# Routing tables filled four columns at a time, an earlier place in the load queue for the input projection's first columns, and a key-norm spread by transposes

## The chip, the core and the metric

The kernel runs on one NeuronCore of one Trainium2 chip. A core has a matrix engine (TensorE, PE in the rows), a vector engine (VectorE, DVE), an activation engine (ScalarE, ACT), a general engine (GpSimd, POOL), and a sync engine (SyncE, SP) that issues most of the transfers. The metric is the device time of one execution in microseconds; lower is better.

## The reference

One layer over 1024 tokens of width 1024: an adaptive norm, one input projection whose columns feed two mixers (a recurrent one with 8 heads and a sparse attention with 8 heads), an output projection, then an adaptive norm and a mixture of 32 experts of which every token takes 2, and a last adaptive norm.

```python
shift1, scale1, gate1, shift2, scale2, gate2 = jnp.split(c_act @ ada_w[l] + ada_b[l], 6, axis=-1)
h = modulate(rms_norm(x, norm1_g[l]), shift1, scale1)
proj = h @ w_in[l]
...
kk = heads(k * k_k)                                   # recurrent mixer: the key, per head
kk = kk / jnp.maximum(jnp.sqrt(jnp.sum(kk * kk, axis=-1, keepdims=True)), 1e-12)
...
order = jnp.argsort(expert)                           # experts: the assignments, sorted by expert
counts = jnp.bincount(expert, length=N_EXPERTS)
padded = (counts + MOE_BLOCK - 1) // MOE_BLOCK * MOE_BLOCK
pend = jnp.cumsum(padded)
dest = (pend - padded)[s_exp] + jnp.arange(n_assign) - start[s_exp]
row_tok = jnp.zeros((n_rows,), jnp.int32).at[dest].set(s_tok)
```

## The kernel before

The program is one straight list of instructions for each engine, with semaphores between them (`sig` raises one, `wait_ge(*at(...))` waits for it, `link` raises one and lets the same engine wait for it). `step` is a `link` of an engine to itself, so that a chain of `step`s is strictly one after the other. There are four stages.

**Project.** SP queues the 8 tiles of x, then the first two of eight conditioning vectors' weights: `load_vector(0)` into slots 0 and 1 of four weight slots, `load_vector(1)` into slots 2 and 3, 2 MB each slot. PE turns x into `hT`, multiplies the conditioning vector by both (`ada`, signal `ada_done`), and DVE and ACT apply scale and shift to `hT` in 16 pieces of 512 columns (`h_even` on DVE, `h_odd` on ACT; the first four of each are the first half of the tokens). Meanwhile `load_group(0)` fetches the first 452 columns of `w_in` into slot 0 in two transfers, 68 columns (`narrow_loaded`) and 384 columns. It waits until PE has read slot 0, and for the landing of the second vector (`slot_loaded3`). The first projection (L801, "rows", one group of 16 matmuls for each of 8 token tiles) needs both transfers and the first half of `hT`; from then on PE works through the other column groups, and DVE, ACT and POOL search the top 256 keys of each query with what it gives. POOL builds constants in this time, among them `steps`, and issues the small loads once the second vector is there. The stage ends with a barrier of all engines.

**Mix.** Eight token tiles of 128 are worked off one after the other. `prepare(t)` normalizes the keys of the next tile: POOL makes the reciprocal norms, DVE spreads them over the head's columns in `rnb` (L1178), PE brings them from rows to columns in bank T1 (L1400, `kk_spread`), DVE multiplies (L1184). Just ahead of that PE turns the values into bank T0 (L1395), ACT empties T0 (L1042), and just behind it PE writes the gate into T0 (L1405). The stage ends with a barrier.

**Route.** Output projection, second norm, choice of the experts. At its end a chain without other work: PE sums up ranks and counts (`ranks`, L1903); DVE works out how many blocks of 32 rows each expert gets (at least 2), each assignment's place `dest`, and two tables: `in_row` (16 columns of tokens x 32) and `in_block` (16 x 132). PE multiplies them (L1907, signal `rows_found`), which gives the token in each row of each block. DVE turns that into the row indices `idx_all` (`indices_ready`), and POOL gathers the first blocks' rows with them. `first_block` holds the first block of every expert (`bounds_ready`).

**Experts.** The blocks go through gate, up and down projections on PE (L2181, L2192). SP loads the 6 MB of an expert into one of three slots as soon as PE has finished with the expert that was in it. Then both rows of each token are added and normalized.

```python
if g == 0:                                            # load_group, SP
    sp.wait_ge(*at("slot_loaded3", "ada", 1))
...
step(dve.tensor_tensor(more, over(counts, SEQ // BLK - 2), each(steps[:, :], NE), ALU.is_gt))
step(dve.tensor_reduce(last, more, AX_X, ALU.add))
```

Of the kernel before, what the change touches and what calls it, by code (L numbers as in the profile page):

```python
# [27 lines left out]
P = 128  # L28
# [24 lines left out]
BLK = 32  # L53
QUARTERS = P // BLK
QD = D // QUARTERS
SLOTS = 3
MAX_BLOCKS = 2 * NE + 2 * SEQ // BLK
# [81 lines left out]
def sparse_attention_moe_layer(nc, x, c, ada_w, ada_b, norm1_g, w_in, shift_mu, w0, w_decay_up, a0, w_aaa_up,  # L139
# [3 lines left out]
    with ExitStack() as ctx:  # L143
        def sb(name, shape, dt=F32):
            return ctx.enter_context(nc.sbuf_tensor(name, shape, dt))
# [52 lines left out]
        steps = sb("steps", [P, SEQ // BLK - 2])  # L198
# [54 lines left out]
        with ExitStack() as scope:  # L253
# [68 lines left out]
            def _(sp):  # L322
# [22 lines left out]
                def load_group(g):  # L345
# [5 lines left out]
                    if g == 0:  # L351
                        sp.wait_ge(*at("slot_loaded3", "ada", 1))
# [36 lines left out]
            def _(pool):  # L389
# [75 lines left out]
                for i in range(SEQ // BLK - 2):  # L465
                    step(pool.memset(steps[:, i:i + 1], float(BLK * (i + 2))))
# [375 lines left out]
        with ExitStack() as scope:  # L842
# [474 lines left out]
            def _(pe):  # L1317
# [59 lines left out]
                def prepare(t):  # L1377
# [21 lines left out]
                    for p in range(NPAIR):  # L1399
                        mm = pe.matmul(g4(psum["T1"])[:, p, :], g4(rnb)[:, p, :], ident[:, :], start=True, stop=True)  # L1400
# [215 lines left out]
        with ExitStack() as scope:  # L1616
# [19 lines left out]
            more, nblk, last, begin = A.take(NE, SEQ // BLK - 2), A.take(NE + 1), A.take(NE), A.take(NE)  # L1636
# [88 lines left out]
            def _(dve):  # L1725
# [98 lines left out]
                step(dve.tensor_copy(first_block[:, 0:NE + 1], nblk))  # L1824
                blocks, pairs = first_block[:, NE:NE + 1], first_block[:, NE + 1:NE + 2]
                step(dve.tensor_scalar(pairs, blocks, 1, None, ALU.bitwise_and))
                step(dve.tensor_tensor(blocks, blocks, pairs, ALU.add))
                step(dve.tensor_scalar(pairs, blocks, 1, None, ALU.logical_shift_right))
                dve.tensor_scalar(first_block[:, NE + 2:NE + 3], pairs, 2, None, ALU.subtract).then_inc(bounds_ready, 1)
                dve.wait_ge(bounds_ready, 1)  # L1830
# [13 lines left out]
                step(dve.tensor_tensor(in_row, over(place_f[0], BLK), each(count_f[:, 0:BLK], 2 * NT), ALU.is_equal))  # L1844
                step(dve.tensor_tensor(in_row, in_row, over(pair_f.rearrange("p t j -> p (t j)"), BLK), ALU.mult))
# [142 lines left out]
            def _(pool):  # L1988
# [6 lines left out]
                for j in range(2):  # L1995
                    gather_first(j)
# [275 lines left out]
```

## Time and profile before

| | |
|---|---|
| median of 3 runs | 1739.64 us (1739.58 to 1743.02) |
| the profiled execution, its own time | 1740.19 us |
| its span (first to last instruction) | 1738.4 us |
| granted TensorE clock, mean over the span | 0.93 of full speed |
| PE busy, share of the span | 87% |
| DVE, ACT, POOL busy, share of the span | 50%, 33%, 26% |

The profile is of one execution. Busy shares are means over stages with different limits, so each stage is read by itself. In a row of the timeline the first number is when a run of alike instructions starts (us from the span's start), the second how long it lasts in all, and the brackets hold the idle time of that engine ahead of it and what ended it. "PEld" is the weight load of PE, "SPq" an issue of a transfer by SP.

### The profile page before, as it was taken

To read this page: it belongs to the slowest core of one execution; us is meant where nothing else is said; L and a number is where in the kernel's file an instruction comes from. 1 tells how busy PE (TensorE), PEld (TensorE's weight loads), DVE (VectorE), ACT (ScalarE), POOL (GpSimd) and SP (SyncE) were. 2 spreads that over 40 slices of the span, in tenths; PEclk is the share of its full clock that TensorE was granted. 3 is DMA by queue.
4 is the path that set the end of the run, shared out by engine and by line. 5 is a ranking of instruction groups with operands and counts; after the bars stand their busy time and mean duration, and the time that the engine had idled before them with its cause. 6 is when DMAs were issued, how large, how long until landed. Compare 5 with 4: busy or idle time off the path is not lost. (4 is left out here: it accounts for less than half of the span.)

```text
span 1738.4 us, 45781 instructions
## 1 busy us (share of the span) xinstructions
PE 1511.5 (87%) x18148; PEld 933.1 (54%) x18149; DVE 874.5 (50%) x1937; ACT 567.4 (33%) x1264; POOL 450.7 (26%) x971
## 2 busy tenths in 40 slices
PE   4799999986778788788889999579889999999976
PEld 3644444434566666666667455535445555555542
DVE  3347578534467766867765332623223333333327
ACT  3212897761324344445445121111111111111122
POOL 6500457740101110110110000033333333343331
PEclk9899999998778898899899999589999999999998
DMA  9613443232020211011003473579999999999945
GB/s 325 209 37 130 173 179 115 93 133 85 1 41 24 86 48 41 14 41 42 8 27 105 145 266 109 218 262 405 408 407 407 392 400 379 406 407 365 407 165 241
DMA packets 136144, 336.71 MB, mean 194 GB/s; under 512 B 14500, under 2 KB 56748, under 8 KB 134992
## 3 DMA queue, kind: packets, MB, share of 16 engines
q1 hardware_dynamic: 126752, 316.09, 48.4%
q0 software_dynamic: 9264, 18.86, 3.2%
q8 instruction: 87, 1.43, 0.3%
q14 instruction: 41, 0.34, 0.1%
HBM read 303.09 MB, written 37.25 MB: 196 GB/s over the span
## 5 line engine op out<-in xcount | busy, mean ns | idle before, releaser
L2181 PE MATMUL psX<-arena 128*32 128x256 f32 x5376 | 331.2, 387 | 15.4 <-DMA arena<-in_e_up_dram 10.4
L2181 PEld LDWEIGHTS psX<-arena 128*32 128x32 f32 x5376 | 166.9, 111 | 136.0 <-issue 43.0
L2192 PE MATMUL psP<-arena 128*32 128x256 f32 x2688 | 160.7, 379 | 10.1 <-issue 9.6
L523 ACT ACTIVATE arena<-arena 128x1024 bf16<-128x1024 f32 (+5 forms) x138 | 134.4, 974 | 31.1 <-POOL arena L481 27.2
L824 PE MATMUL psX<-arena 128*128 128x512 f32 x320 | 140.9, 595 | 3.5 <-DVE arena L730 2.0
L824 PE MATMUL psP<-arena 128*128 128x512 f32 x320 | 141.2, 595 | 3.1 <-DVE arena L730 1.6
L2091 DVE TENSOR_TENSOR arena<-arena,pair_cols 128x256 f32<-128x256 f32 x85 | 36.2, 426 | 199.6 <-PE psX L2181 199.6
L2192 PEld LDWEIGHTS psP<-arena 128*32 128x32 f32 x2688 | 88.3, 110 | 68.7 <-issue 14.7
L2052 ACT ACTIVATE arena<-psX 64x256 f32<-64x256 f32 x84 | 31.7, 378 | 251.8 <-PE psX L2181 251.8
L2011 POOL DMA_INDIRECT arena<-xn_rows,arena x84 | 88.3, 1051 | 74.0 <-POOL arena L2008 70.5
L2021 POOL DMA_INDIRECT expert_rows<-arena x84 | 85.8, 1021 | 74.1 <-POOL arena L2018 74.1
L824 PEld LDWEIGHTS psP<-arena 128*128 128x128 f32 x320 | 59.9, 190 | 80.2 <-issue 75.4
L824 PEld LDWEIGHTS psX<-arena 128*128 128x128 f32 x320 | 60.0, 190 | 78.9 <-issue 73.7
L2085 DVE TENSOR_TENSOR arena<-psT,pair_cols 128x256 f32<-128x256 f32 x85 | 36.1, 425 | 119.7 <-PE psT L2159 119.7
L479 POOL TENSOR_SCALAR arena<-arena 128x1 f32<-128x1 f32 x132 | 58.3, 441 | 145.8 <-ACT arena L523 138.7
L2056 ACT ACTIVATE arena<-psW 128x128 f32<-128x128 f32 x84 | 23.3, 278 | 209.9 <-PE psW L2164 209.9
L952 POOL TENSOR_TENSOR st<-st,mhalf 128x8 f32<-128x8 f32 x16 | 29.1, 1818 | 174.6 <-DVE st L1193 91.4
L1531 PE MATMUL psW<-arena 64*64 64x64 f32 x1280 | 51.4, 237 | 22.9 <-DVE arena L1273 22.8
L1147 DVE CUSTOM_DVE_ANT_0 arena<-psP,arena 128x384 f32<-128x384 f32 (+5 forms) x48 | 42.8, 891 | 53.9 <-PE psP L1330 53.0
L1531 PEld LDWEIGHTS psW<-arena 64*64 64x64 f32 x1280 | 46.0, 150 | 33.0 <-DVE arena L1273 29.8
L2008 POOL COPY arena<-idx_all 128x1 int32 (+1 forms) x84 | 15.6, 186 | 185.5 <-ACT arena L2048 185.5
L980 POOL TENSOR_TENSOR arena<-arena,ident 128x512 f32<-128x512 f32 x8 | 9.0, 1123 | 206.9 <-DVE arena L1297 183.7
(442 smaller groups left out, 2723.9 us busy)
## 6 DMA issues: line engine op xcount, KB each, us to landing
arena<-in_e_gate_dram SPq DMA_DIRECT2D x32, 2048.0 KB, 14.2
arena<-in_e_up_dram SPq DMA_DIRECT2D x32, 2048.0 KB, 18.3
arena<-in_e_down_dram SPq DMA_DIRECT2D x32, 2048.0 KB, 17.2
arena<-in_ada_w_dram SPq DMA_DIRECT2D x12, 2048.0 KB, 14.3
proj_T<-arena SPq DMA_DIRECT2D x36, 256.0 KB, 2.0
arena<-in_x_dram SPq DMA_DIRECT2D x16, 512.0 KB, 6.5
arena<-in_w_in_dram SPq DMA_DIRECT2D x4, 2048.0 KB, 9.0
arena<-in_final_ada_w_dram SPq DMA_DIRECT2D x4, 2048.0 KB, 10.3
```

The costliest lines, as they stand in the source:

```text
L479: step(pool.tensor_scalar(s_hit[k], s_sum[k], s_lim[k], s_step[k][:, i - 1:i], ALU.is_gt, ALU.mult))
L523: link(act, act.activation(junk_bf[:, 0:n], score[k][:, 0:n], ACT.Sign, scale=s_sgn[k], bias=s_neg[k], accum_out=s_sum[k]), "counted", k, i)
L824: mm = pe.matmul(psum[b], w[:, k, first:first + P], hT[:, k, 512 * half:512 * half + 512], start=(k == 0), stop=(k == KD - 1))
L1147: link(dve, dve.tensor_tensor_reduce(two(lg[:, h % 2, 0:n]), two(psum["P"])[:, :, 0:n // 2], two(mask), 1.0, BEYOND, ALU.add, ALU.min, s_l ...
L1531: mm = pe.matmul(by_q(f"W{g}", CHUNK)[part(c_), p, :], TT[part(c_), g, 1, p, :], Xs[part(c_), g, p, :], start=True, stop=True)
L2011: pool.indirect_dma_start(rows_in[j], None, xn2_d[:, :], bass.IndirectOffsetOnAxis(ap=index_now[j], axis=0), bounds_check=QUARTERS * SEQ - ...
L2021: pool.indirect_dma_start(y_d[:, :], bass.IndirectOffsetOnAxis(ap=place_now[j], axis=0), y_sb[j], None, bounds_check=QUARTERS * 2 * SEQ - ...
L2052: act.activation(tanh_g, gate_ps, ACT.Tanh, scale=0.5).then_inc(q("tanh_done"), 1)
L2085: dve.tensor_tensor(xs, rows_ps, of_pairs(1), ALU.mult).then_inc(q("xs_ready"), 1)
L2091: dve.tensor_tensor(xT, xs, of_pairs(0), ALU.add).then_inc(q("xT_ready"), 1)
L2181: mm = pe.matmul(psum["X0"][BLK * c_:BLK * c_ + BLK, 0:DE // 2], xT[:, r, g, :], w[:, 2 * g + r, DE // 2 * h:DE // 2 * (h + 1)], start=(j ...
L2192: mm = pe.matmul(psum["P0"][BLK * g:BLK * g + BLK, 0:QD], hidT[:, f, h, :], down_w[u][:, KE // 2 * h + f, QD * g:QD * g + QD], start=(i == ...
```

## The change

There are three parts.

1. `load_group(0)` no longer waits for the landing of the second vector; the wait for PE's reading of slot 0 stays. 
2. `kk_spread` is done by `pe.transpose` instead of `pe.matmul` against the identity.
3. The end of the route stage. Block counts come from integer arithmetic (add 31, shift by 5, at least 2), and the constant `steps` with its 30 memsets on POOL is gone. `first_block` is written behind the tables. The tables are filled four columns at a time, with a signal for each four, and PE waits for each. The indices of the first two blocks are made ahead of those of the other 130, each with a step of `indices_ready`; POOL waits for the second step behind its two first gathers.

```diff
                     if g == 0:
-                        sp.wait_ge(*at("slot_loaded3", "ada", 1))
...
-                for i in range(SEQ // BLK - 2):
-                    step(pool.memset(steps[:, i:i + 1], float(BLK * (i + 2))))
...
-                        mm = pe.matmul(g4(psum["T1"])[:, p, :], g4(rnb)[:, p, :], ident[:, :], start=True, stop=True)
+                        mm = pe.transpose(g4(psum["T1"])[:, p, :], g4(rnb)[:, p, :], ident[:, :])
...
-                step(dve.tensor_tensor(more, over(counts, SEQ // BLK - 2), each(steps[:, :], NE), ALU.is_gt))
-                step(dve.tensor_reduce(last, more, AX_X, ALU.add))
-                step(dve.tensor_scalar(last, last, 2.0, None, ALU.add))
+                step(dve.tensor_scalar(count_blocks, counts, float(BLK - 1), None, ALU.add))
+                step(dve.tensor_scalar(count_blocks, count_blocks, 5, None, ALU.logical_shift_right))
+                step(dve.tensor_scalar(last, count_blocks, 2.0, None, ALU.max))
...
+                for i in range(0, 2 * NT, PLACED):
+                    some = slice(i, i + PLACED)
+                    step(dve.tensor_tensor(in_row[:, some], over(place_f[0][:, some], BLK), each(count_f[:, 0:BLK], PLACED), ALU.is_equal))
+                    step(dve.tensor_tensor(in_row[:, some], in_row[:, some], over(pair_of[:, some], BLK), ALU.mult))
+                    link(dve, dve.tensor_tensor(in_block[:, some], over(place_f[1][:, some], ALL_BLOCKS), each(count_f, PLACED), ALU.is_equal), "in_block", i)
...
-                pe.wait_ge(*at("in_block", 0))
                 for i in range(2 * NT):
+                    if i % PLACED == 0:
+                        pe.wait_ge(*at("in_block", i))
```

On SP, at the start of the program, the order of the issues stays and one wait goes. Before (the names in brackets are semaphores; `ada_done` is PE's reading of the first vector):

```order
L335 DMA arena<-in_ada_w_dram 128x4x1024 x2
L327 DMA arena<-in_ada_b_dram 32x256 x4
L354 DMA arena<-in_w_in_dram 128x8x68 [waits project_slot_loaded3,project_ada_done]
L355 DMA arena<-in_w_in_dram 128x8x384
L359 DMA arena<-in_w_in_dram 128x8x512 [waits project_slot_loaded0,project_ada_done]
```

And now:

```order
L335 DMA arena<-in_ada_w_dram 128x4x1024 x2
L327 DMA arena<-in_ada_b_dram 32x256 x4
L353 DMA arena<-in_w_in_dram 128x8x68 [waits project_ada_done]
L354 DMA arena<-in_w_in_dram 128x8x384
L358 DMA arena<-in_w_in_dram 128x8x512 [waits project_slot_loaded0,project_ada_done]
```

The two transfers of `w_in` can be issued while the second vector (the first row) is still being moved.

On DVE, at the end of the route stage, the first rows behind the counts. Before (`psW` holds the counts, `first_block` the bounds):

```order
L1819 TENSOR_TENSOR arena<-psW,steps 128x960
L1820 TENSOR_REDUCE arena<-arena 128x32
L1821 TENSOR_SCALAR arena<-arena 128x32
L1822 MEMSET arena 128x1
L1823 SCALAR_TENSOR_TENSOR arena<-ones,arena 128x32
L1824 CAST first_block<-arena 128x33
L1826 TENSOR_SCALAR first_block<-first_block 128x1
L1827 ISA first_block<-first_block 128x2
L1828 TENSOR_SCALAR first_block<-first_block 128x1
L1829 TENSOR_SCALAR first_block<-first_block 128x1
L1831 TENSOR_SCALAR arena<-arena 128x32
```

And now, up to the same instruction (L1831 is now L1821):

```order
L1816 TENSOR_SCALAR arena<-psW 128x32
L1817 TENSOR_SCALAR arena<-arena 128x32
L1818 TENSOR_SCALAR arena<-arena 128x32
L1819 MEMSET arena 128x1
L1820 SCALAR_TENSOR_TENSOR arena<-ones,arena 128x32
L1821 TENSOR_SCALAR arena<-arena 128x32
```

Two instructions over 960 elements are gone, and the five on `first_block` have moved down.

Further down on DVE, the tables and the first indices. Before (`in_row` twice, `in_block`, then the indices from PE's result in `psW`):

```order
L1844 TENSOR_TENSOR arena<-arena 128x512
L1845 TENSOR_TENSOR arena<-arena 128x512
L1846 TENSOR_TENSOR arena<-arena 128x2112
L1849 TENSOR_SCALAR place_all<-psW 128x132
L1850 TENSOR_SCALAR idx_all<-place_all 128x132
L1851 TENSOR_SCALAR idx_all<-idx_all 128x2
L1852 TENSOR_SCALAR idx_all<-idx_all,quarter 128x132
```

And now, from the last of the four pieces on:

```order
L1837 TENSOR_TENSOR arena<-arena 128x128
L1838 TENSOR_TENSOR arena<-arena 128x128
L1839 TENSOR_TENSOR arena<-arena 128x528
L1840 CAST first_block<-arena 128x33
L1842 TENSOR_SCALAR first_block<-first_block 128x1
L1843 ISA first_block<-first_block 128x2
L1844 TENSOR_SCALAR first_block<-first_block 128x1
L1845 TENSOR_SCALAR first_block<-first_block 128x1
L1850 TENSOR_SCALAR place_all<-psW 128x2
L1851 TENSOR_SCALAR idx_all<-place_all 128x2
L1852 TENSOR_SCALAR idx_all<-idx_all 128x2
L1853 TENSOR_SCALAR idx_all<-idx_all,quarter 128x2
```

The first three rows stand there four times in all; the five on `first_block` now stand between the tables and the reading of PE's result, which begins with two columns.

## Rows read from the trace of the kernel before

**Rows 1.** The page: its first line, and the chain that ended last.

```profile
span 1738.4 us, 45781 instructions
...
PE 34%; DMA 4%; DVE 3%; issue 1%; SPq 1%; ACT 0%; POOL 0%; POOLq 0%; DVEq 0%; ACTq 0%
```

**Rows 2.** Windows: busy us of each engine, granted clock, DMA share, GB/s.

```profile
52.70:56.60 3.90, 3.89 (x13) 3.90 (x14) 0.00 (x0) 0.00 (x0) 3.26 (x14) 0.54 0.81 165
56.60:409.80 353.20, 338.54 (x1241) 159.77 (x1239) 207.51 (x529) 194.37 (x388) 135.47 (x466) 1.00 0.35 126
440.00:975.00 535.00, 440.71 (x7466) 344.50 (x7463) 357.89 (x725) 223.69 (x490) 54.00 (x39) 0.89 0.14 40
1140.10:1686.10 546.00, 519.75 (x8400) 298.50 (x8400) 177.75 (x420) 82.02 (x255) 204.53 (x334) 0.98 0.95 375
```

**Rows 3.** Timeline of the start.

```profile
26.10 1.93 PE L766 MATMUL psW<-arena 128*32 128x256 f32 x32 [0.38 <-DMA arena<-in_ada_w_dram]
...
38.92 0.58 SPq L355 DMA_DIRECT2D arena<-in_w_in_dram  x1
...
43.43 5.75 ACT L508 ACTIVATE arena<-arena,mod_cols 128x512 f32<-128x512 f32 x8 [18.89 <-DVE mod_cols L595]
...
52.71 23.23 PE L801 MATMUL psT<-arena 128*128 128x196 f32 x128 [9.85 <-DMA arena<-in_w_in_dram]
...
77.92 2.94 POOL L472 TENSOR_TENSOR arena<-arena,mhalf 128x16 f32<-128x16 f32 x1 [10.60 <-DVE arena L631]
```

**Rows 4.** Windows around the gap in the transfers, columns as in rows 2.

```profile
36.00:37.00 1.00, 0.34 (x8) 0.00 (x0) 0.00 (x0) 0.00 (x0) 0.00 (x0) 1.00 0.45 116
37.00:39.00 2.00, 0.54 (x12) 0.37 (x16) 0.00 (x0) 0.00 (x0) 0.01 (x1) 1.00 0.04 14
40.00:42.00 2.00, 1.39 (x16) 0.30 (x8) 0.46 (x2) 0.00 (x0) 2.00 (x5) 0.50 1.12 320
```

**Rows 5.** Timeline of the mix stage: the first tile's spread, then the third tile's.

```profile
434.81 1.77 PE L1400 MATMUL psT<-ident,arena 128*128 128x128 f32 x8 [4.38 <-DVE arena L1178]
...
554.29 0.66 PE L1395 MATMUL psT<-ident,arena 128*128 128x128 f32 x4
...
554.79 1.06 PE L1400 MATMUL psT<-ident,arena 128*128 128x128 f32 x8
555.05 0.60 ACT L1042 ACTIVATE arena<-psT 128x512 f32<-128x512 f32 x1 [1.14 <-PE psT L1395]
...
555.79 1.10 PE L1405 MATMUL psT<-wgate,arena 128*128 128x512 f32 x2
```

**Rows 6.** Timeline of the end of the route stage.

```profile
1112.51 1.16 DVE L1819 TENSOR_TENSOR arena<-psW,steps 128x960 f32<-128x960 f32 x1 [1.49 <-PE psW L1903]
...
1116.47 0.18 DVE L1831 TENSOR_SCALAR arena<-arena 128x32 f32<-128x32 f32 x1
...
1119.66 0.69 DVE L1844 TENSOR_TENSOR arena<-arena 128x512 f32<-128x512 f32 x1
...
1121.11 2.36 DVE L1846 TENSOR_TENSOR arena<-arena 128x2112 f32<-128x2112 f32 x1
...
1123.52 6.01 PE L1907 MATMUL psW<-arena 128*32 128x132 f32 x128 [11.11 <-DVE arena L1846]
1129.68 0.30 DVE L1849 TENSOR_SCALAR place_all<-psW 128x132 int32<-128x132 f32 x1 [6.21 <-PE psW L1907]
...
1131.67 1.23 POOL L1991 DMA_INDIRECT arena<-xn_rows,idx_all  x1 [41.65 <-DVE idx_all L1852]
...
1137.88 0.42 ACT L2048 ACTIVATE arena<-arena 128x256 f32<-128x256 f32 x1 [28.58 <-DMA arena<-xn_rows,idx_all]
```

**Rows 7.** Line L335, the loads of the vectors' weights: from issue to landing.

```profile
DMA to landing us min/median/max: 7.6/12.9/24.4
```

**Rows 8.** Timeline of PE's first transposes, eight at a time.

```profile
13.89 1.94 PE L786 MATMUL psT<-ident,arena 128*128 128x128 f32 x8 [13.89 <-DVE arena L614]
...
20.20 1.04 PE L786 MATMUL psX<-ident,arena 128*128 128x128 f32 x8
```

More of the change, by code:

```diff
@@ L56 @@
 SLOTS = 3
+PLACED = 4
 MAX_BLOCKS = 2 * NE + 2 * SEQ // BLK
@@ L197, in sparse_attention_moe_layer @@
         halves = sb("halves", [P, MANTISSA])
-        steps = sb("steps", [P, SEQ // BLK - 2])
         quarter = sb("quarter", [P, 1])
@@ L1635, in sparse_attention_moe_layer @@
             gm, pg, v1, v2, e2, den = (A.take(NT) for _ in range(6))
-            more, nblk, last, begin = A.take(NE, SEQ // BLK - 2), A.take(NE + 1), A.take(NE), A.take(NE)
+            count_blocks, nblk, last, begin = A.take(NE).bitcast(I32), A.take(NE + 1), A.take(NE), A.take(NE)
             RS, picked, destf = A.take(NT, NE), A.take(NT, 2, NE), A.take(NT, 2)
@@ new lines, in _ @@
+                step(dve.tensor_copy(first_block[:, 0:NE + 1], nblk))
+                blocks, pairs = first_block[:, NE:NE + 1], first_block[:, NE + 1:NE + 2]
+                step(dve.tensor_scalar(pairs, blocks, 1, None, ALU.bitwise_and))
+                step(dve.tensor_tensor(blocks, blocks, pairs, ALU.add))
+                step(dve.tensor_scalar(pairs, blocks, 1, None, ALU.logical_shift_right))
+                dve.tensor_scalar(first_block[:, NE + 2:NE + 3], pairs, 2, None, ALU.subtract).then_inc(bounds_ready, 1)
@@ L1847, in _ @@
+                dve.wait_ge(bounds_ready, 1)
                 dve.wait_ge(*at("rows_found", 0))
                 found = psum["W1"][:, 0:ALL_BLOCKS]
-                step(dve.tensor_scalar(place_all[:, :], found, float(NO_PAIR), None, ALU.add))
-                step(dve.tensor_scalar(idx_all[:, :], place_all[:, :], 1, None, ALU.logical_shift_right))
-                step(dve.tensor_scalar(idx_all[:, 0:2], idx_all[:, 0:2], SEQ - 1, None, ALU.min))
-                dve.tensor_scalar(idx_all[:, :], idx_all[:, :], float(QUARTERS), quarter[:, 0:1], ALU.mult, ALU.add).then_inc(indices_ready, 1)
+                first = slice(0, 2)
@@ new lines, in _ @@
+                step(dve.tensor_scalar(place_all[:, first], found[:, first], float(NO_PAIR), None, ALU.add))
+                step(dve.tensor_scalar(idx_all[:, first], place_all[:, first], 1, None, ALU.logical_shift_right))
+                step(dve.tensor_scalar(idx_all[:, first], idx_all[:, first], SEQ - 1, None, ALU.min))
+                dve.tensor_scalar(idx_all[:, first], idx_all[:, first], float(QUARTERS), quarter[:, 0:1], ALU.mult, ALU.add).then_inc(indices_ready, 1)
+                rest_of = slice(2, ALL_BLOCKS)
@@ L1853, in _ @@
+                step(dve.tensor_scalar(place_all[:, rest_of], found[:, rest_of], float(NO_PAIR), None, ALU.add))
+                step(dve.tensor_scalar(idx_all[:, rest_of], place_all[:, rest_of], 1, None, ALU.logical_shift_right))
+                dve.tensor_scalar(idx_all[:, rest_of], idx_all[:, rest_of], float(QUARTERS), quarter[:, 0:1], ALU.mult, ALU.add).then_inc(indices_ready, 1)
                 step(dve.tensor_scalar(place_all[:, :], place_all[:, :], float(QUARTERS), quarter[:, 0:1], ALU.mult, ALU.add))
@@ L1996, in _ @@
                     gather_first(j)
+                pool.wait_ge(indices_ready, 2)
                 pool.wait_ge(bounds_ready, 1)
```

11 lines of the change are left out of this document (1 added, 10 removed).

## The prediction

> **What bounds the kernel now.** I read the page first: its span, and the chain of work that ended last. The chain reaches back over less than half of the span; of that PE makes up 34% of the span, and all other engines and the transfers together some 9% [rows 1]. The reader should take from it that PE, in order, sets the end, and that an edit on another engine counts only where PE stands still. Next the windows, one for each stage [rows 2]. Between 56.6 and 409.8 us PE is busy 338.5 of 353.2 us at full granted clock; in the mix stage 440.7 of 535 at 0.89; among the experts 519.8 of 546 at 0.98, with the transfers at 375 GB/s. So a stage behind a late start is nearly full, and moving the start moves its end. Then the timeline at the three places that the diff touches.
>
> At the start PE stands still for 9.85 us, until the first columns of `w_in` are there at 52.71, though ACT has finished its first half of `hT` (four of eight pieces in 5.75 us from 43.43, so 43.43 + 2.88 = 46.3) [rows 3]. The second of the two loads of these columns is issued at 38.92, after the second vector has landed. The windows show what that order costs: from 36 to 37 the transfers fall to 116 GB/s, and until 39 they move 14 GB/s [rows 4]. The data of the vector is in; the queue is empty until SP has heard of it and the next load has started.
>
> In the mix stage the spread takes PE about 1 us a tile, between two uses of bank T0 [rows 5]. At the end of the route stage nothing overlaps: DVE from 1112.51, PE from 1123.52, DVE from 1129.68, POOL's gather at 1131.67, and ACT has the rows at 1137.88 [rows 6].
>
> **The start.** PE has read slot 0 at 26.10 + 1.93 = 28.03 [rows 3]. The new wait is over then, and both loads can be issued some 10 us ahead of 38.92. I take it that the queue works in the order of issue, since a vector's load took up to 24.4 us to land where the shortest took 7.6 [rows 7]: it stood behind others. Then the columns start where the vector's data ends, about 36.5. They are 452 x 1024 x 4 B = 1.85 MB. At the 320 GB/s that two streams together moved from 40 to 42 [rows 4] that is 5.8 us, to 42.3; with 2.4 us from last data to use, as from 36.5 to 38.9 before, 44.7. If POOL's small loads, which still start when the vector lands, take half of it from 40 on, 1.12 MB are in by then, the other 0.73 MB at 160 GB/s take 4.6, and they are usable at 47.0. The bound that replaces them is `hT` at 46.3, which this edit does not move. So PE starts between 46.3 and 47.0 instead of 52.71: 5.7 to 6.4 us. I take **6.2**, near the end without sharing, because most is moved before 40. PE's low clock at its start (granted 0.54 from 52.7 to 56.6 [rows 2]) stays and may last one or two us longer or shorter, so the bounds are 4.7 to 7.4. What waits behind SP's two issues is the next column group, needed only after the rows (23.23 us of PE); it comes earlier too. The 30 memsets that go lie on POOL ahead of L472, where POOL waits 10.60 us for DVE; DVE now comes 6.2 earlier, which leaves 4.4 without counting the memsets. They count nothing; without that cover they would hold the reciprocal norms.
>
> **The spread.** Four blocks are 8 records as a matmul (L1400) and 4 as a transpose (L1395 turns four blocks of the same shape). From start to start that is 1.00 us for L1400 (554.79 to 555.79) and 0.50 for L1395 (554.29 to 554.79) [rows 5]. Eight tiles would give 8 x 0.5 = 4 us, a little more in the first, where 8 records took 1.77 at the low clock. But what follows, L1405, writes the bank that ACT's L1042 is emptying, and that ends at 555.05 + 0.60 = 555.65, only 0.14 ahead of L1405's start at 555.79. ACT's copy hangs on L1395, which is not moved. So 0.1 us a tile at most gets through there, and PE then waits for ACT instead. In the first tile the bank is long free: half of 1.77, of which I count 0.5, since the clock rises later. Lower bound nothing, upper 4.4; I take **0.8**, near the low end, because the wait is in the rows.
>
> **The route stage's end** [rows 6]. From L1819's start to L1831's are 3.96 us. In place of that stand five small instructions; L1831, on the same 32 columns, took 0.18, and a gap is some 0.035 (L1844 and its like behind it take 0.69 each, and L1846 starts 1.45 behind L1844), so five take 1.1: 2.9 us less. L1831 to L1844 stays 3.19, so the tables begin at 1112.51 + 1.1 + 3.2 = 1116.8. For a piece: 512 elements took 0.69 and 2112 took 2.36, so 1.04 ns an element and 0.16 fixed; 128, 128 and 528 elements take 0.29 + 0.29 + 0.71, and three gaps of 0.03 make 1.38. All four are 5.5 instead of 3.8, but PE starts at 1118.2 and not behind them. Its 6.01 us for 128 records are 1.5 a piece, more than DVE's 1.38, so it is not starved, and ends at 1124.2 (before: 1129.53). The five instructions on `first_block` come at 1122.3 and are done by about 1123.4, under PE's last piece; were they not covered they would cost 1. Behind PE were 1.99 us from L1849 to the gather; four instructions on 2 columns instead of 132 save some 0.3. So the gather goes at 1126.0 instead of 1131.67, 5.7 earlier. ACT's rows came 6.2 later, while 2 MB of an expert's down weights, which SP issues on the same signal as DVE's L1849, were on the way; if they set the landing, it moves by 5.3. I take **5.5**, bounds 4.5 (PE waits a little at each piece) to 6.3 (PE's clock rises before its end). The second step of `indices_ready` comes about 1 us behind the first, under POOL's 1.23 us on the first gather; behind POOL's new wait stand only the gathers of later blocks, which wait for ACT anyway, and behind PE's new waits only the rest of the tables.
>
> **The sum.** 6.2 + 0.8 + 5.5 = 12.5 us, against the profiled execution's 1740.19: 1727.7. The median of the runs is 0.55 below that execution, so **1727** there. Between the places I let everything move as a block: loads of later columns and of experts wait for PE's progress, not for a time.
>
> **Rivals.** (a) *The columns share with the second vector.* Then it lands later by up to the columns' 5.8 us, and `hT` with it: 46.3 + 5.8 = 52.1, a gain of 0.6 to 2. Total 6.9 to 8.3, 1731 to 1733. For it: no row shows two such loads in one queue at this place. Against: the 24.4 us. (b) *The saved half of the spread gets through*, if L1042 comes earlier with everything else: 3.6 more, 1723.5. Against: the 0.14 us. (c) *The experts' weights give the last part back*, as waits of PE on a stream that is nearly full (0.95): total 7, 1732.5. Against: that stream starts with PE's release of the first slot, so it moves along. (d) *Slower: the clock.* The mix stage runs at 0.89 of the clock, so it falls there already. If less PE work per tile lets it fall once or twice more in each, for as long as at the start (3.9 us [rows 2]), with PE busy for 0.82 of that (440.7 of 535) at half speed, a fall costs 3.9 x 0.82 / 2 = 1.6 us, and eight tiles 13 to 26: 1740 to 1753. It decides from 12.5 / 8 = 1.6 us a tile on. On transposes the rows say: eight took 1.94 us at 13.89 and 1.04 at 20.20, with no other kind of PE work since the start [rows 8], so transposes alone brought the clock from 1.2 to 2.4 GHz. The Trainium skill (TensorE: Matmul & The Clock Gate, section Part 4: PE-mode transpose) says the contrary, that the transpose mode doesn't count as busy in the same way and doesn't bring the full clock. By that rule the stretch of the spread would be lost to the clock, and (d)'s 1740 would be the likelier time; the rows don't bear it out.
>
> **How the numbers follow.** My forecast 0.74, with a range of its own of 1723 to 1731 (the three terms' bounds, of which not all end on one side); (a) 0.13, (b) 0.05, (c) 0.05, (d) 0.03. The range 1722.5 to 1733 holds the forecast, (a), (b) and (c) but for their edges, and leaves out (d). 0.2% of the time, 3.5 us, is about what a measurement of this kernel tells from no change; 1736.2 is that line. All but (d) lie below it: faster 0.94, same 0.04, slower 0.02, the last two from (d) and from mishaps that I have not thought of.
>
> **What would show it.** Right: L801 starts at 46.3 to 47 and its wait names ACT's or DVE's piece of `hT`; no gap in the transfers from 36 to 39; PE's rows of the tables start 5.6 us behind the counts, not 11; the gather about 13.5 us behind them instead of 19.2; tile for tile, L1405 starts within 0.1 us of ACT's L1042 and the mix stage keeps its length within 1 us; the experts' stage keeps its 546 us. Wrong: the second vector lands later than 38.5; PE idles between the pieces; the granted clock of the mix stage leaves 0.89 by 0.03 or more; PE's waits for weights grow by what the route stage saved.

## The result, and the profile after

| | before | after |
|---|---|---|
| median of 6 runs each | 1739.66 us (1735.98 to 1745.84) | 1728.67 us (1726.49 to 1731.77) |
| the profiled execution: own time, span | 1740.19, 1738.4 us | 1726.49, 1724.8 us |

The ratio is 0.9933, with a 95% interval of 0.9912 to 0.9954: 11.7 us shorter, between 8 and 15. The two profiled executions differ by more, 13.6 us of span; the profile of after is of the fastest of its six runs, and a part of that difference will turn out not to belong to the change.

**The start.** Timeline of the changed kernel (columns as in [rows 3]; L798 was L801, L505 was L508, and L354, L358 are SP's issues of the first and of the next columns):

```profile
28.54 6.48 SPq L354 DMA_DIRECT2D arena<-in_w_in_dram  x1
...
38.74 3.29 PE L763 MATMUL psW<-arena 128*32 128x256 f32 x32 [2.13 <-DMA arena<-in_ada_w_dram]
...
43.85 5.75 ACT L505 ACTIVATE arena<-arena,mod_cols 128x512 f32<-128x512 f32 x8 [19.21 <-DVE mod_cols L592]
...
46.77 0.37 SPq L358 DMA_DIRECT2D arena<-in_w_in_dram  x1
...
47.04 15.17 PE L798 MATMUL psT<-arena 128*128 128x196 f32 x76 [3.76 <-ACT arena L505]
```

PE's rows start at 47.04 instead of 52.71, and the wait ahead of them now names ACT's piece of `hT`. SP's next issue, which waits for the columns, stands at 46.77, so the columns were there just before: the two bounds lie close together. By the packets in the trace the data of the columns move from 36.0 to 45.7 us (39.5 to 51.9 before) and those of the second vector until 38.1 (37.9 before). The windows around the old gap, the start of PE's rows, the mix and the experts' stage (columns as in [rows 2]):

```profile
36.00:37.00 1.00, 0.61 (x8) 0.00 (x0) 0.00 (x0) 0.00 (x0) 0.00 (x0) 0.50 1.21 210
37.00:39.00 2.00, 0.26 (x4) 0.20 (x8) 0.00 (x0) 0.00 (x0) 0.00 (x0) 0.50 1.17 292
40.00:42.00 2.00, 2.00 (x24) 0.79 (x16) 0.00 (x0) 0.00 (x0) 2.00 (x5) 0.61 1.07 377
47.00:49.50 2.50, 2.46 (x8) 2.49 (x9) 1.82 (x4) 2.50 (x4) 2.50 (x5) 0.50 0.90 175
49.50:56.00 6.50, 6.50 (x34) 6.50 (x33) 0.72 (x2) 1.34 (x8) 6.18 (x12) 0.82 1.06 255
435.00:967.00 532.00, 435.89 (x7429) 340.96 (x7423) 357.56 (x726) 221.60 (x486) 54.58 (x39) 0.89 0.14 40
1126.60:1672.00 545.40, 519.11 (x8396) 299.06 (x8388) 177.56 (x420) 81.17 (x253) 203.28 (x332) 0.98 0.96 375
```

Where the transfers moved 14 GB/s [rows 4] they now move 292. The mix and the experts' stage read as before [rows 2].

**The mix stage,** third tile, timeline of after (L1392, L1397, L1039, L1402 were L1395, L1400, L1042, L1405; L1580 was L1583):

```profile
548.10 0.66 PE L1392 MATMUL psT<-ident,arena 128*128 128x128 f32 x4
548.59 0.60 PE L1397 MATMUL psT<-ident,arena 128*128 128x128 f32 x4
548.85 0.60 ACT L1039 ACTIVATE arena<-psT 128x512 f32<-128x512 f32 x1 [1.80 <-PE psT L1392]
...
549.59 1.10 PE L1402 MATMUL psT<-wgate,arena 128*128 128x512 f32 x2 [0.40 <-ACT arena L1039]
...
559.31 0.34 PE L1580 MATMUL psT<-arena 64*64 64x64 f32 x8 [1.20 <-issue]
```

The spread has 4 records instead of 8 and lasts 0.60 us instead of 1.06 [rows 5], and a new wait for ACT, 0.40 us, stands behind it. L1402 starts 1.49 behind L1392; before it was 1.50 (554.29 to 555.79). Nothing of the saved half came through in this tile.

**The end of the route stage,** timeline of after, to be held against [rows 6]:

```profile
1104.50 0.19 DVE L1816 TENSOR_SCALAR arena<-psW 128x32 int32<-128x32 f32 x1 [1.48 <-PE psW L1908]
...
1105.54 0.18 DVE L1821 TENSOR_SCALAR arena<-arena 128x32 f32<-128x32 f32 x1
...
1110.14 5.33 PE L1913 MATMUL psW<-arena 128*32 128x132 f32 x128 [5.76 <-DVE arena L1839]
...
1115.63 0.16 DVE L1850 TENSOR_SCALAR place_all<-psW 128x2 int32<-128x2 f32 x1 [0.38 <-PE psW L1913]
...
1117.35 1.23 POOL L1997 DMA_INDIRECT arena<-xn_rows,idx_all  x1 [35.34 <-DVE idx_all L1857]
...
1123.63 0.42 ACT L2055 ACTIVATE arena<-arena 128x256 f32<-128x256 f32 x1 [22.34 <-DMA arena<-xn_rows,idx_all]
```

From the counts to L1821 1.04 us instead of 3.96, PE starts 5.64 behind the counts instead of 11.01, the gather is 12.85 behind them instead of 19.16.

**By stage.** The boundaries are the starts of the rows (L801 before), of the last projection's last record (L824), of the mix stage's L1390, of the last record of the ranks (L1903) and of ACT's rows (L2048); the "head" is what lies between the last projection and L1390. "Lost clock" is the time in the mix stage multiplied by what the granted clock lacks of full speed, from the trace's record of that clock, of which the PEclk of a window is the rounded mean.

| us | to rows | projections | head of mix | mix, output, route | lost clock there | end of route | experts, tail |
|---|---|---|---|---|---|---|---|
| before | 52.71 | 351.1 | 18.3 | 689.9 | 75.3 | 25.87 | 600.6 |
| after | 47.04 | 351.5 | 15.95 | 689.5 | 73.4 | 19.64 | 601.1 |
| after less before | -5.67 | +0.4 | -2.3 | -0.5 | -1.9 | -6.23 | +0.6 |

The 2.3 us at the head, where ACT waits for the first load of `proj_T`, were in nobody's sum. The experiments settle whose they are.

### The profile page after: what moved, and what is told of

The parts are those of the page before. It is cut to its first block and busy times, and to the rows that moved or that the text cites. A ratio compares the mean times of both kernels' runs of the same rounds, so it can differ in the third digit from the quotient of the medians.

```text
span 1724.8 us, 45699 instructions
## 1 busy us (share of the span) xinstructions
PE 1508.2 (87%) x18116; PEld 929.4 (54%) x18117; DVE 873.6 (51%) x1949; ACT 566.9 (33%) x1264; POOL 447.5 (26%) x941
## 5 line engine op out<-in xcount | busy, mean ns | idle before, releaser
L821 PEld LDWEIGHTS psX<-arena 128*128 128x128 f32 x320 | 60.0, 190 | 78.9 <-issue 73.6
## 6 DMA issues: line engine op xcount, KB each, us to landing
arena<-in_ada_w_dram SPq DMA_DIRECT2D x12, 2048.0 KB, 14.8
```

Source lines behind the costliest of these rows:

```text
L821: mm = pe.matmul(psum[b], w[:, k, first:first + P], hT[:, k, 512 * half:512 * half + 512], start=(k == 0), stop=(k == KD - 1))
```

## The experiments

The kernel before ran beside each, so ratios are to it, with their 95% intervals. Its own median lay between 1739.7 and 1744.0 us in the four sets, so kernels of different sets are compared by their ratios. The next table takes the profiles of all of them by the same boundaries; the readings below go back to it.

| kernel | median us | ratio to before | to rows | head | mix, output, route | lost clock | end of route | experts, tail |
|---|---|---|---|---|---|---|---|---|
| part 1 alone | 1738.39 | 0.9980 (0.9964-0.9997) | 46.90 | 17.95 | 694.7 | 81.1 | 25.66 | 601.3 |
| part 2 alone | 1739.94 | 0.9995 (0.9982-1.0008) | 52.33 | 18.06 | 690.1 | 73.7 | 25.58 | 601.3 |
| part 3 alone | 1735.02 | 0.9966 (0.9949-0.9983) | 52.19 | 18.14 | 687.6 | 74.1 | 19.38 | 600.7 |
| tables in one piece | 1731.34 | 0.9946 (0.9925-0.9967) | 46.84 | 18.09 | 689.9 | 73.6 | 22.50 | 601.7 |
| part 1 taken back | 1733.84 | 0.9947 (0.9930-0.9964) | 52.14 | 18.59 | 690.1 | 73.7 | 19.61 | 603.9 |
| memsets back | 1728.19 | 0.9915 (0.9895-0.9935) | 47.31 | 18.01 | 687.5 | 67.3 | 19.61 | 604.3 |
| spread fourfold | 1729.47 | 0.9915 (0.9891-0.9940) | 46.13 | 17.93 | 693.7 | 67.0 | 19.66 | 600.6 |
| spread twelvefold | 1762.03 | 1.0113 (1.0091-1.0134) | 46.56 | 17.73 | 725.0 | 65.5 | 19.33 | 600.6 |
| spread as products | 1764.50 | 1.0142 (1.0119-1.0164) | 47.06 | 18.14 | 725.0 | 72.4 | 19.43 | 600.9 |
| one filler | 1725.60 | 0.9901 (0.9884-0.9918) | 47.26 | 17.96 | 687.2 | 58.6 | 19.44 | 599.8 |
| two fillers | 1720.27 | 0.9873 (0.9849-0.9897) | 46.72 | 18.44 | 683.4 | 51.6 | 20.80 | 602.7 |
| two fillers, transposes | 1718.86 | 0.9871 (0.9851-0.9891) | 47.05 | 18.89 | 680.0 | 49.9 | 19.40 | 600.5 |

**Part 1 alone,** the kernel before with

```diff
                     if g == 0:
-                        sp.wait_ge(*at("slot_loaded3", "ada", 1))
```

> The kernel before with part 1 alone: load_group(0) no longer waits for the second vector. Theory (the start is a block shift, what is saved stays): the rows start 5.5 to 6 us earlier, their wait is for the piece of hT and not for the columns, the last projection ends 5 to 6 us earlier, and the whole is 5 to 6 us shorter; everything behind the mix stage's head is moved by one and the same amount. Rival 1 (the columns take their time from the second vector): the vector lands 2 us or more later than 38.5 us and the gain is below 2 us. Rival 2 (the 2.3 us which the changed kernel gained at the head of the mix stage, where ACT waits for the first rows of proj_T, come from this part, because the loads stand otherwise in the queue): the whole is 7 to 8.5 us shorter, and ACT's wait for proj_T is 2 us shorter than before. If that gain is only how one execution happened to fall, the wait is as long as before here, or is short in kernels that don't touch the start.

Measured: 1738.39 us, 0.5 to 6.3 us shorter, less than the theory's middle. In its profile the rows start at 46.90, behind ACT's piece again, and the last projection comes 5.3 us earlier; but the mix stage is 4.8 us longer than before. Windows from the fourth tile's values (L1395, here L1394) to the fifth's, here and then in the kernel before:

```profile
611.11:675.93 64.82, 53.46 (x912) 42.92 (x908) 44.57 (x93) 25.99 (x59) 6.65 (x5) 0.84 0.13 33
```

```profile
614.78:676.78 62.00, 50.62 (x913) 40.68 (x909) 44.77 (x93) 25.68 (x58) 6.65 (x5) 0.89 0.13 34
```

The same instructions, 2.8 us more, and the granted clock is 0.84 for 0.89. Part 1 by itself doesn't make this tile longer: in the three other kernels with the early start and without added records (after, tables in one piece, memsets back) it takes 61.8 to 62.2 us. So where the clock's low stretches lie shifts a tile by some us from one execution to another. The rival that the columns take their time from the vector is out: the vector's products start at 38.27, no later than before. The head took 17.95 us, as without the change: rival 2 is out too.

**Part 2 alone,** the kernel before with `pe.transpose` in `kk_spread`.

> The kernel before with part 2 alone: kk_spread as a transpose. Theory (PE's saved half is handed to the wait for ACT's copy of the bank, which L1405 writes): 0.3 to 0.8 us shorter in all, all of it in the first tile; in the seven others the spread takes 0.5 us instead of 1.0 and PE's wait ahead of L1405 grows by the same 0.5; not to be told from no change in the time. Rival 1 (the saved half gets through): 3.5 to 4.4 us shorter. Rival 2 (a transpose doesn't keep the clock up, by the Trainium skill, TensorE: Matmul & The Clock Gate, section Part 4: PE-mode transpose): the granted clock of the mix stage falls from 0.89 by 0.03 or more and the time grows by 13 us or more. Neither touches the loads at the head of the mix stage: a shorter wait of ACT there by 2 us would say that this wait varies by itself.

Measured: no change that can be told. From L1395 to L1583, the next place at which PE stands still, the tiles took these times (us), read from the starts in the timelines:

| | first tile, to the products behind the spread (L1445) | third to eighth tile, to L1583 |
|---|---|---|
| before | 6.74 | 11.22, 11.65, 12.08, 13.04, 13.23, 14.12 |
| part 2 alone | 5.64 | 11.22, 11.64, 12.08, 13.04, 13.23, 14.12 |
| after | 5.94 | 11.22, 11.64, 12.08, 13.04, 13.23, 14.12 |
| spread fourfold (16 records) | 8.69 | 11.89, 12.31, 12.75, 13.71, 13.90, 14.79 |
| spread twelvefold (48) | 12.12 | 15.38, 15.81, 16.24, 17.20, 17.39, 18.28 |

Half of the records gone is worth 0.01 us at most in a tile at full clock, and 0.8 to 1.1 in the first. Up to L1583 the first tile takes 75.9 to 76.5 us in the three profiles with products and 75.3 to 75.9 in the five with four transposes and no filler, on the mean 76.2 and 75.5. In a tile the saving is below what the time can tell.

**Part 3 alone,** the changed kernel with the two other edits taken back:

```diff
+                        sp.wait_ge(*at("slot_loaded3", "ada", 1))
...
-                        mm = pe.transpose(g4(psum["T1"])[:, p, :], g4(rnb)[:, p, :], ident[:, :])
+                        mm = pe.matmul(g4(psum["T1"])[:, p, :], g4(rnb)[:, p, :], ident[:, :], start=True, stop=True)
```

> The kernel before with part 3 alone: integer block counts, tables in four pieces, first indices ahead of the others, no steps memsets. Theory (all of it lies on the one chain at the end of the route stage): from the counts to the gather 12.8 to 13.7 us instead of 19.2, 5.5 to 6.3 us shorter; the experts' stage keeps its length within 1 us, and the whole is 5 to 6.3 us shorter. Rival (the experts' weight stream gives it back): the gather is earlier by the same, but PE's waits for weights among the experts grow by 4 us or more, and the whole is under 2 us shorter. The head of the mix stage is not touched here either.

Measured: 5.9 us shorter (3 to 8.9), the gather 12.79 behind the counts (1109.89 to 1122.68), the experts' stage as before. The theory holds; the weight stream gave nothing back.

**Tables in one piece,** the changed kernel with

```diff
-PLACED = 4
+PLACED = 16
```

> The changed kernel with the tables in one piece of sixteen columns (PLACED 16) in place of four pieces of four; all else as in the changed kernel. By the prediction's steps the counts give 2.9 us, the first two indices 0.3, and the pieces the rest. Theory (PE begins behind the first piece and DVE is done with each further piece before PE needs it): with one piece PE's rows of the tables start 8 us or so behind the counts instead of 5.6, the gather 15.0 to 15.9 us behind them instead of 12.85, so this kernel is 2.0 to 2.9 us slower than the changed one and 8.5 to 10 us faster than the one before. Rival (PE's rows run at the low clock because they start early, so the pieces only trade a wait of PE for slower rows): the 128 records take less than 4.7 us in one piece, and the gather is less than 1.5 us later than in the changed kernel.

Measured: by the ratios 2.3 us above the changed kernel, with intervals that overlap, so the rows decide. Timeline of the three that matter:

```profile
1106.16 0.19 DVE L1816 TENSOR_SCALAR arena<-psW 128x32 int32<-128x32 f32 x1 [1.49 <-PE psW L1908]
...
1114.25 5.83 PE L1913 MATMUL psW<-arena 128*32 128x132 f32 x128 [8.20 <-DVE arena L1839]
...
1121.95 1.22 POOL L1997 DMA_INDIRECT arena<-xn_rows,idx_all  x1 [38.26 <-DVE idx_all L1857]
```

PE starts 8.09 behind the counts, and the gather stands 15.79 behind them instead of 12.85. The pieces are worth 2.9 us: PE starts 2.45 earlier and takes 0.5 less. The counts (2.92), the first indices (0.27) and PE's 5.83 us for 6.01 are the other 3.4 of 6.3. PE's rows were not faster for starting later (5.83 against 5.33), so the rival is out.

**Part 1 taken back,** the changed kernel with the wait in `load_group(0)` again.

> The changed kernel with part 1 taken back (load_group(0) waits for the second vector again); parts 2 and 3 stay. Part 1 alone was worth 3.5 us (0.5 to 6.3), while its profile showed 5.3 us at the end of the projections and all but 0.9 of it lost again in the first five tiles of the mix stage, where the granted clock was low for longer than in the other profiles. Theory (the start is worth its 5.2 us on the mean; what the mix stage adds or takes is where the clock falls in one execution): this kernel is 4 to 6.5 us slower than the changed one, which runs beside it as the kernel with the memsets put back; if its profile is shorter or longer by more, the tiles whose length differs are the tiles whose low clock differs, at about 0.55 us of length for 1 us of lost clock. Rival (an earlier start is systematically given back in the mix stage): 0.5 to 3 us slower than the changed one.

Measured: 1733.84 against 1728.19 of the kernel beside it (next), 5.6 us, and by the ratios 2.4 above the changed kernel. With part 1 alone (3.5) there are three differences between 2.4 and 5.6, each with an interval of some 3 us or more on both sides. They hold the profile's 5.2; a small part given back in the mix stage is not excluded.

**Memsets back,** the changed kernel with

```diff
+                for i in range(SEQ // BLK - 2):
+                    step(pool.memset(steps[:, i:i + 1], float(BLK * (i + 2))))
```

> The changed kernel with the constant steps and its 30 memsets back on POOL, used by nobody. Theory (POOL waits 10 us for DVE behind them): no change, within 1 us of the changed kernel's 1728.7, so about 0.993 of the kernel before; in the profile POOL's wait ahead of the reciprocal norms is shorter than the changed kernel's by what the memsets take, 1 to 3 us, and the norms start at the same distance from PE's rows. Rival (they hold the norms or the small loads, and with them the start): the first projection 1 us or more later against the rows' start, 1 to 3 us slower. It serves as the changed kernel for the others of this call.

Measured: 1728.19. Timeline of POOL in this kernel:

```profile
60.94 4.62 POOL L466 MEMSET steps<- 128x1 f32 x30
...
73.18 2.93 POOL L472 TENSOR_TENSOR arena<-arena,mhalf 128x16 f32<-128x16 f32 x1 [5.61 <-DVE arena L631]
```

The 30 take 4.62 us, more than I had expected, and POOL still waits 5.61 for DVE behind them (9.96 in the changed kernel). They cost nothing, so this kernel stands for the changed one in its set. Its profile was longer than that of after for other reasons: 2.1 us at the head and 3.1 among the experts. There PE waited for the up weights as follows, in the changed kernel and then here (us in total, times, longest):

```profile
PE psX L2188 <- DMA arena<-in_e_up_dram: 10.8, 5, 4.7
```

```profile
PE psX L2191 <- DMA arena<-in_e_up_dram: 13.7, 5, 4.7
```

**Spread fourfold,** the changed kernel with

```diff
-                    for p in range(NPAIR):
-                        mm = pe.transpose(g4(psum["T1"])[:, p, :], g4(rnb)[:, p, :], ident[:, :])
+                    for p in range(4 * NPAIR):
+                        mm = pe.transpose(g4(psum["T1"])[:, p % NPAIR, :], g4(rnb)[:, p % NPAIR, :], ident[:, :])
```

> The changed kernel with the spread's four transposes written four times over (16 records in place of 4, the same values). Theory (the saving of part 2 vanished because PE waits for ACT's copy of the bank anyway, so a longer spread is free only up to that copy's end): in a tile at full clock the spread takes about 2.0 us in place of 0.6, the write behind it starts 0.9 to 1.1 us later and no longer right behind ACT; 7 to 13 us slower than the changed kernel, the first tile's 3 us at the low clock among them. Rival 1 (DVE's and ACT's later waits have room, so that PE makes it up at its next wait for DVE): under 4 us slower. Rival 2 (by the Trainium skill, TensorE: Matmul & The Clock Gate, section Part 4: PE-mode transpose, transposes don't count as busy): the granted clock of the mix stage drops below that of the changed kernel by 0.02 or more, and the loss is above 13 us.

Timeline of the third tile:

```profile
550.28 0.66 PE L1392 MATMUL psT<-ident,arena 128*128 128x128 f32 x4
550.78 1.91 PE L1397 MATMUL psT<-ident,arena 128*128 128x128 f32 x16
551.04 0.60 ACT L1039 ACTIVATE arena<-psT 128x512 f32<-128x512 f32 x1 [1.85 <-PE psT L1392]
...
552.52 1.02 PE L1402 MATMUL psT<-wgate,arena 128*128 128x512 f32 x2
```

L1402 no longer waits for ACT, which ended at 551.64, and starts 2.24 behind L1392, 0.75 more than in the changed kernel. By the table above a tile at full clock takes 0.67 longer, the first 2.75, and the second, whose clock is partly low, 1.3: some 8 us in all. In the profiles the mix stage is 6.2 us longer than in the kernel with memsets, at the same lost clock (67.0 and 67.3). The time shows none of it (1729.47, the same ratio as the kernel with memsets), but its six runs lie between 1720.5 and 1733.4, further apart than those of any other kernel here, so they don't exclude a cost of some us. My theory's 7 to 13 us is not borne out by the time; the place at which the cost arises, behind ACT's copy, is in the rows. The size is left to the next kernel.

**Spread twelvefold,** the same with `12 * NPAIR`.

> The changed kernel with the spread's transposes written twelve times over (48 records, same values). Fourfold, the time was 0 to 4 us above the changed kernel's, though in its profile the mix stage was 6.2 us longer at the same lost clock. Theory (free only up to ACT's copy, about 4 records more; behind that each record costs its 0.12 us): 48 records are 5.8 us a tile at full clock, 4.9 to 5.2 more than free, 40 to 46 us in eight tiles with the first at a lower clock. Rival 1 (PE makes up what it loses at its next waits for DVE and ACT, some 1 us a tile): 30 to 38 us. Rival 2 (transposes let the clock fall): more than 50 us, with a lost clock of the mix stage of 80 us or more.

Measured: 1762.03, some 31 us above the changed kernel by the ratios and 34 above the kernel with memsets. The tiles at full clock take 4.16 longer, not 4.9 to 5.2, the first 6.2, the second 4.9: some 36 us, as the mix stage (35.5). So removing four records gives nothing, adding twelve costs 0.67 us in such a tile, and the next thirty-two 3.5, or 0.109 each: the slack ends at ACT's copy. My theory's sum was too high, and the time is in rival 1's range, but not for its reason: L1402 starts 5.73 behind L1392 instead of 1.49, 4.24 later, and L1580 is still 4.16 later, so PE makes up hardly anything on the way.

**Spread as products,** the same with `6 * NPAIR` products instead of transposes, 48 records again.

> The changed kernel with the spread as products by the identity again, six times over: 48 records, as many as in the twelvefold transposes. Theory (a transpose record and a product record cost the same and keep the clock alike, so part 2 is worth its records alone): within 3 us of the twelvefold transposes, lost clock of the mix stage within 6 us of theirs. Rival (transposes don't count as busy, the rule of the Trainium skill, TensorE: Matmul & The Clock Gate, section Part 4: PE-mode transpose): 8 us or more faster than the transposes, with 15 us or more of lost clock less.

Measured: 1764.50, by the ratios some 5 us (0 to 10) above the twelvefold transposes, 2.5 by the medians, with 6.9 us more of lost clock: at or a little beyond my bounds, and to the other side than the rival's. A transpose is no worse for the clock than a product here.

**One filler,** the changed kernel with products that nobody reads, ahead of PE's wait for DVE at the fourth level (`fill` waits until the bank is free, and moves up with them):

```diff
+                            if l == 4 and g == 0:
+                                fill(pe, "W0", "tt", t, l, g)
+                                for i in range(6):
+                                    pe.matmul(g4(psum["W0"])[:, i % 4, :], ident[:, :], ident[:, :], start=True, stop=True)
```

> The changed kernel with six matrix products of the identity by itself (12 records, about 1.4 us at full clock and 2.8 at half) put in PE's longest wait for DVE in each mix tile (2.3 to 3.6 us ahead of the fourth level, five or six of the eight tiles), into a bank that is written anew right behind them; what is computed stays the same. Theory (the clock falls in the mix stage because PE stands still there, and where it falls sets that stage's length): the granted clock of the mix stage rises by 0.02 or more over 0.89, low stretches behind those waits go, and the kernel is 3 to 10 us faster than the changed one. Rival 1 (the clock falls for other reasons, such as the many products of 64 by 64, which leave most of the array idle, and not for these waits): the clock stays within 0.01 and the time within 2 us. Rival 2 (the filler runs at half clock and holds the level behind it): 2 to 8 us slower.

Measured: 1725.60, 2.6 us below the kernel with memsets, and the intervals of the two ratios still overlap. Lost clock 58.6 instead of the 65 to 81 of the kernels without filler; from 435 to 967 us the granted clock is 0.92 instead of 0.89, so rival 1, which left it within 0.01, is out. The direction is the theory's, its size not decided.

**Two fillers,** the same and one more at the start of each tile:

```diff
                     mm.then_inc(*sig("ak_done", t))
+                    fill(pe, "X0", "square", t, 0)
+                    for i in range(6):
+                        pe.matmul(g4(psum["X0"])[:, i % 4, :], ident[:, :], ident[:, :], start=True, stop=True)
```

> The changed kernel with the filler of six products of the identity (12 records) at two places of each mix tile: ahead of the fourth level, as before, and ahead of the second head's products, where PE waits 1.8 to 4.4 us for DVE in every tile. With the first place alone the lost clock of the mix stage fell to 58.6 us from 67 to 73 and the time was 0.990 of the kernel before. Theory (PE's standing still lets the clock fall, and where it falls sets the length of the mix stage): lost clock below 52 us, time 0.985 to 0.989 of the kernel before. Rival 1 (the first place took all that the waits cost, since the second place's tiles run at full clock already): 0.988 to 0.992, lost clock 55 to 62 us. Rival 2 (the first filler's gain was chance): 0.991 to 0.995.

Measured: 0.9873, within the theory's range, though its interval reaches into rival 1's; lost clock 51.6, where rival 1 had 55 or more. **Two fillers, transposes,** twelve `pe.transpose` for the six products at each place:

> The same two fillers as twelve transposes of the identity each in place of six products: as many records, of the same length. Theory (a transpose keeps the clock up as a product does, as the first rows of the profile say, where transposes alone halved their own duration): lost clock of the mix stage within 4 us of the kernel with two fillers of products, time within 0.002 of its ratio. Rival (the Trainium skill, TensorE: Matmul & The Clock Gate, section Part 4: PE-mode transpose: the transpose mode doesn't count as busy): lost clock as in the changed kernel without filler or more, 67 us and up, and no gain over it.

Measured: 1718.86, 0.9871. Timeline of its filler ahead of the fourth level, the second of eight:

```profile
534.92 1.53 PE L1525 MATMUL psW<-ident 128*128 128x128 f32 x12
...
538.57 1.15 PE L1537 MATMUL psW<-arena 64*64 64x64 f32 x32 [2.12 <-DVE arena L1270]
```

The same place in the changed kernel:

```profile
539.76 1.89 PE L1528 MATMUL psW<-arena 64*64 64x64 f32 x32 [3.57 <-DVE arena L1270]
```

The wait of 3.57 us now holds 1.53 us of filler, and the 32 products behind it take 1.15 us instead of 1.89. (In the profile of before they took 1.15 as well: it depends on where an execution's low stretches lie.) Windows of the mix, output and route with the two fillers, and then in the changed kernel (the third number from the end is the granted clock):

```profile
417.63:1097.59 679.96, 589.39 (x8180) 434.06 (x8178) 422.63 (x878) 252.81 (x552) 61.95 (x52) 0.93 0.24 76
```

```profile
414.54:1103.99 689.45, 580.79 (x7988) 426.26 (x7986) 421.31 (x878) 252.81 (x552) 61.73 (x52) 0.89 0.23 75
```

PE is busy 8.6 us longer, and the stretch takes 9.5 us less. By the ratios this kernel takes 1.3% less time than the kernel before and 0.6% less than the changed one (0.4% less than the kernel with memsets). The lost clock is that of the products within 1.7 us. The Trainium skill (TensorE: Matmul & The Clock Gate, section Part 4: PE-mode transpose) says that the transpose mode doesn't count as busy in the same way; these two pairs of kernels, whose transposes are of f32, don't agree with it, and the measurement decides.

## Why the prediction was right, step by step

The forecast was 1727.0 in a range of 1722.5 to 1733; it is 1728.67. The kernel with memsets, which is the changed kernel but for them, measured 14.8 us less than the kernel before (11 to 18), the changed kernel 11.7 (8 to 15): the forecast of 12.5 lies in both. The mechanisms of all three parts were right, each term a little off. That the sum is this near has luck in it: the start came out 1.0 below its term and the route's end 0.7 to 0.8 above, and the two cancel.

- **The start, 6.2.** It measured 5.67 at the rows and 5.2 at the last projection. The bound was right in this profile (`hT`), and the gap in the transfers went. What failed is the size: ACT began 0.42 later than in the profile of before, and 0.3 us pass between ACT's fourth piece (43.85 + 2.88 = 46.73) and PE's start, which the sum left out. The 0.5 behind it is the low clock at PE's start, granted 0.50 from 47.0 to 49.5 and 0.82 to 56.0: 2.4 us of clock are lost up to the last projection instead of 1.8. I had counted it as one or two us either way. The estimate that the columns are there at 44.7 without sharing was too early: 46.77 is nearer to the 47.0 of the sharing case. The vector's data ended at 37.9 and not at 36.5, and the columns took 9.7 us, not the 5.8 to 8.1 of the sum. So the columns bind as soon as `hT` is early. The second vector's 32 products took 1.93 us at a granted clock of 1.00 (fourfold) and 3.64 at 0.50 (one filler), and ACT began at 42.1 and 44.1. With the early start PE began 0.01 to 0.02 us behind SP's next issue, and so with the columns, in three of ten profiles: 46.84 (one piece), 46.13 (fourfold), 46.56 (twelvefold).
- **Rival (a)** is refuted: the second vector's products start at 38.74 instead of 38.46, and ACT's start varied between 42.0 and 44.1 in all the profiles, with the wait and without it.
- **The spread, 0.8.** 0.8 to 1.1 in the first tile (0.8 up to L1583), 0.01 in each of the others at full clock; the term had 0.5 and 0.3 for them. The reason was right as well: L1402 follows ACT's copy by 0.14 us before and after. Rival (b) is refuted by the same rows.
- **The route's end, 5.5.** 6.2 to 6.3, the upper bound, by the mechanism that had been named for it: the clock rose before PE's end (granted 1.00 from 1114.0 to 1115.5, where it was 0.85 in PE's last 2 us before), and its 128 records took 5.33 instead of 6.01. Counts 2.92 (2.9 foreseen), PE 5.64 behind the counts (5.6), first indices 0.27 (0.3).
- **Rival (c)** is refuted: with part 3 alone the experts' stage took 600.7 us, and its 600 to 604 in all profiles don't follow the route's gain. **Rival (d)** is refuted: the granted clock stays at 0.89, and records taken from the spread or added to it as transposes did not lower it.
- **"Everything between moves as a block"** was the step that holds at most on the mean. The mix stage was between 687.5 and 694.7 us long in the kernels without filler or added records, with a lost clock of 67 to 81. The head's 2.3 us were in the profile of after alone: in every other profile the head took 17.7 to 18.9 us. They are one execution's, not the change's, and without them the two profiles differ by 11.3 us, the ratio's 11.7.

Whether an earlier start is in part given back in the mix stage stays open: 2.4 to 5.6 us in time against 5.2 in the profiles, with intervals as wide as the difference. The eight profiles without filler or added records show little of it: that stage takes 690.4 us on the mean of the four with the early start and 689.4 on that of the four without.

## What to carry to other kernels

Before counting a shorter step as a gain, look for the other engine whose result the next step needs: here ACT's copy ended 0.14 us ahead of PE's next write, and with half of the spread's records gone nothing was gained in a tile at full clock, while more of them cost. Compare stages between several profiles, not one pair, before a difference of 2 or 3 us is explained. And where PE waits for 2 to 4 us in a stage with a granted clock below full, work that nobody reads, placed in the wait, can be worth more than the removal of real work: 8 to 11 us for two fillers here by the ratios, against some 1 for the spread's records.

## What the runs showed of the hardware that was not expected

- SP stood 6.48 us on the single issue L354 at 28.54, while the second vector was still being moved; in the kernel before, the same issue at 38.92 took 0.58. It is 6.5 to 6.6 in all ten profiles with the early start, and 0.58 in all four without. The transfer's data began to move at 37.4, just ahead of the vector's last at 38.1, with no gap.
- The clock of the mix stage answers to work placed in PE's waits: two fillers of 1.5 us a tile took the lost clock from 73.4 us (67 to 81 in the eight profiles without filler or added records) to 50 to 52 and the stage from 689.5 to 680 to 683, 0.3 to 0.4 us of time for each us of lost clock.
- Transposes held the clock as products did (49.9 and 51.6 us lost with fillers, 65.5 and 72.4 with 48 records in the spread).
